# A hybrid decoder step on one core: sample outputs from the old states with eight buffers, the S5 output in two halves, and the SSD norm between other gate blocks

## What is computed

```
proj = rmsnorm(x) @ w_in                       # z, xBC, dt, u
xBC  = silu(causal_conv(xBC))                  # x, B, C of the SSD heads
y    = ssd(x, dt, A, B, C, D, h0)              # 16 heads of 64, state 128, chunks of 128 tokens
y_ssd = rmsnorm(y * silu(z)) * ssd_norm
y_s5 = s5(u, h0_re, h0_im)                     # 64 groups, diagonal complex state of 64
y_s5 = gelu(y_s5);  y_s5 = rmsnorm(y_s5 * sigmoid(y_s5 @ w_glu + b_glu)) * s5_norm
x    = x + concat(y_ssd, y_s5) @ w_out
x    = x + hier_moe(rmsnorm(x))                # top 2 of 32 experts, d_ff 512
```

```
h = exp(dt*A) * h0 + (dt*x) B^T                # 16 x 64 x 128 per sample: also an output
y = h C + D*x
```

## Time and profile before

| | us |
|---|---|
| median of 3 runs (lowest, highest) | 1232.8 (1232.26, 1233.92) |
| profiled execution, its own time | 1232.51 |
| its span, first to last instruction | 1230.7 |
| PE, DVE, ACT, POOL busy in the span | 1017.0, 399.5, 281.5, 299.4 |
| mean granted TensorE clock, share of full speed | 0.928 |

### The profile page before, as it was taken

The page is one execution under the profiler, slowest core; times in us unless marked ns, Lnnn a source line. Parts: engine busy times, 40 slices in busy tenths (PEclk is TensorE's granted clock), DMA queues, the critical chain, the costliest instruction groups (busy, mean ns, idle before and its releaser), DMA issues.

```text
span 1230.7 us, 16173 instructions
## 1 busy us (share of the span) xinstructions
PE 1017.0 (83%) x6140; PEld 692.2 (56%) x6141; DVE 399.5 (32%) x678; ACT 281.5 (23%) x554; POOL 299.4 (24%) x480
## 2 busy tenths in 40 slices
PE   5999999896999974699964999999976778976760
PEld 3888789675674763577743555555533434543430
DVE  3998374532423328651233101011000001000006
ACT  3125224530222604341121121121201111111102
POOL 1000788884014593035002001010100000000003
PEclk8999999897997896899985999999999999999895
DMA  5685341110057550415464999999999999999976
GB/s 214 241 137 84 75 106 36 37 52 16 29 121 160 188 154 18 161 70 205 171 255 167 384 389 383 389 394 386 394 401 398 400 405 395 385 389 402 390 271 214
DMA packets 83814, 291.19 MB, mean 237 GB/s; under 512 B 33460, under 2 KB 35380, under 8 KB 74940
## 3 DMA queue, kind: packets, MB, share of 16 engines
q1 hardware_dynamic: 69304, 252.97, 57.1%
q0 software_dynamic: 6944, 23.83, 6.3%
q10 hardware_dynamic: 7524, 13.83, 3.1%
HBM read 260.75 MB, written 27.59 MB: 234 GB/s over the span
## 4 chain that ended last, share of the span: by engine, by line
PE 48%; DMA 16%; POOL 15%; DVE 8%; issue 7%; SPq 3%; ACT 1%; DVEq 0%; ACTq 0%; POOLq 0%
DMA sb_arena<-w_up 11%; PE ps L860 9%; PE ps L618 8%; PE ps L957 7%; PE ps L950 7%; PE ps L971 6%; DMA sb_arena<-w_gate 4%; SPq L470 3%; POOL sb_rec L525 2%; POOL sb_rec L526 2%; POOL sb_arena L529 2%; POOL sb_arena L528 2%; POOL sb_rec L527 2%; PE ps L932 2%; PE ps L730 1%
## 5 line engine op out<-in xcount | busy, mean ns | idle before, releaser
L618 PE MATMUL ps<-sb_arena 128*128 128x264 f32 (+1 forms) x1152 | 272.9, 399 | 6.1 <-DVE sb_arena L1330 6.1
L618 PEld LDWEIGHTS ps<-sb_arena 128*128 128x128 f32 x1152 | 224.4, 196 | 55.4 <-issue 12.3
L950 PE MATMUL ps<-sb_arena 128*64 128x256 f32 x1152 | 138.4, 395 | 35.2 <-DMA sb_arena<-w_gate 28.3
L1708 DVE TENSOR_TENSOR sb_sst<-sb_sst,ps 128x256 f32<-128x256 f32 x36 | 15.2, 421 | 450.7 <-PE ps L957 414.0
L971 PE MATMUL ps<-sb_arena 128*64 128x512 f32 x576 | 131.5, 598 | 26.8 <-DVE sb_arena L1713 26.8
L957 PE MATMUL ps<-sb_arena 128*64 128x256 f32 x1152 | 132.9, 384 | 20.9 <-DMA sb_arena<-w_up 20.9
L950 PEld LDWEIGHTS ps<-sb_arena 128*64 128x64 f32 x1152 | 86.3, 143 | 98.4 <-DMA sb_arena<-w_gate 39.5
L957 PEld LDWEIGHTS ps<-sb_arena 128*64 128x64 f32 x1152 | 83.2, 138 | 66.6 <-DMA sb_arena<-w_up 27.1
L581 POOL COPY sb_idc<-sb_idx 64x1 int32 x36 | 6.4, 178 | 439.2 <-ACT sb_arena L1271 439.1
L971 PEld LDWEIGHTS ps<-sb_arena 128*64 128x64 f32 x576 | 38.1, 136 | 97.1 <-issue 61.7
L1274 ACT ACTIVATE sb_kxf<-ps 128x512 f32<-128x512 f32 x36 | 21.5, 597 | 310.5 <-PE ps L971 310.5
(11 more groups left out here) (270 smaller groups left out, 1205.4 us busy)
## 6 DMA issues: line engine op xcount, KB each, us to landing
sb_arena<-w_gate SPq DMA_DIRECT2D x32, 2048.0 KB, 35.0
sb_arena<-w_up SPq DMA_DIRECT2D x32, 2048.0 KB
sb_arena<-w_down SPq DMA_DIRECT2D x32, 2048.0 KB
sb_arena<-wi SPq DMA_DIRECT2D x28, 512.0 KB, 4.1
ye_scr<-sb_kxf ACTq DMA_DIRECT2D x72, 128.0 KB
sb_arena<-w_out SPq DMA_DIRECT2D x4, 2048.0 KB, 8.3
ye_scr<-sb_arena SPq DMA_DIRECT2D x2, 2048.0 KB, 11.9
sb_arena<-wglu SPq DMA_DIRECT2D x8, 512.0 KB, 4.9
```

The costliest lines, as they stand in the source:

```text
L618: last = mm(ps[:, b0 + h, 0:t1 - t0], ring[w % 3][:, k, :], src[:, k, t0:t1], start=k == 0, stop=k == KD - 1)
L950: last = mm(ps[64 * r:64 * r + 64, 0, 0:256], xt[:, k, :], Wg[s][:, k, 256 * r:256 * r + 256], start=k == 0, stop=k == KD - 1)
```

## The change

The output of a sample is formed from its old state: y = exp(dt*A) * (h0 C) + (C.B) * dt*x + D*x. VectorE multiplies the old state by C as soon as it is loaded; only then does GpSimd update the state in place (it waits for `smv_done` of the same sample). All eight states have buffers of their own, loaded at once; the first four lie where ScalarE later writes the sigmoids, which therefore wait for their stores, and the high part of `w_out` waits for the others.

B and C of the samples are transposed behind block 13, copied by ScalarE into a tile of 516 columns, to which VectorE adds C.B; ScalarE's queue stores them to a scratch tensor, and GpSimd's queue loads them broadcast to 128 partitions (8 x 516 floats each) behind the last state output, ahead of the states. Samples 0 and 1 stand on VectorE between chunks 3 and 4.

The S5 output is stored and loaded in halves of 32 groups, the first as soon as half of the additions are done. `Tm` is cleared by VectorE instead of GpSimd. ScalarE takes the exponentials of chunk 0 ahead of the last two SiLUs. The squares of the SSD norm stand behind the sigmoid of block 29 instead of 31, its partition sum behind block 31 instead of 33, and the high parts one block earlier.

The diff without declarations:

```diff
-        h0b = [part(20272 + 1024 * i, 8, NSTATE) for i in range(HB)]
+        h0b = [part((30832 if i < 4 else 16176) + 1024 * i, 8, NSTATE) for i in range(NS)]
+        bcf = part(26416, NS * BCW)
...
@@ sync
-            for w in range(22, 29):
+            for w in range(22, 26):
                 ring_load(w)
-            sp.wait_ge(y5_ev, 16)
...
+            def y_store(half):
+                sp.wait_ge(y5_ev, 8 * half + 8)
+                gs = slice(32 * half, 32 * half + 32)
+                for j in range(J):
+                    sp.dma_start(ydst[j][:, gs], Ug[16 * j:16 * j + 16, gs, 0:NC5]).then_inc(y5_st[half], 16)
+                sp.dma_start(ysdst[:, gs], Ug[0:16, gs, COL_S0:COL_S0 + NS]).then_inc(y5_st[half], 16)
...
+            y_store(0)
+            for w in range(26, 29):
+                ring_load(w)
+            y_store(1)
+            sp.wait_ge(y5_st[0], 16 * 9)
+            y_load(0)
+            sp.wait_ge(y5_st[1], 16 * 9)
+            y_load(1)
@@ gpsimd
-            pl.wait_ge(k_mm, 1)
-            nc.gpsimd.memset(Tm, 0.0).then_inc(t_zero, 1)
...
-            for b in range(HB):
-                pl.dma_start(h0b[b], hin[b]).then_inc(h0s_ld[b], 16)
+            pl.wait_ge(bc_st, 16)
+            pl.wait_ge(s5_out, 32)
+            pl.dma_start(bcf, bc_scr.rearrange("b c -> (b c)").partition_broadcast(P)).then_inc(bc_ld, 16)
             for b in range(NS):
-                hb = h0b[b % HB]
-                pl.wait_ge(bcs_ev, b + 2)
+                pl.dma_start(h0b[b], hin[b]).then_inc(h0s_ld[b // 4], 16)
+            pl.wait_ge(bc_ld, 16)
+            for b in range(NS):
+                hb = h0b[b]
                 link(nc.gpsimd.tensor_tensor(smu.rearrange("p (g i) n -> p g i n", g=2), bc(bcb[b][:, 0:2], 2, 4),
                                              bc(xds[:, :, b].rearrange("p (g i) -> p g i", g=2), 3, NSTATE), ALU.mult))
-                pl.wait_ge(h0s_ld[b % HB], 16 * (b // HB + 1))
+                pl.wait_ge(smv_done, b + 1)
                 link(nc.gpsimd.tensor_tensor(hb, hb, bc(eA[:, :, b], 2, NSTATE), ALU.mult))
...
-                if 1 <= b <= NS - HB:
...
@@ tensor
+            wide(13)
+            pe.wait_ge(silu_done, 4)
+            for i in range(4):
+                last = nc.tensor.transpose(ps[0:24, 7, i * P:(i + 1) * P], xcB[:, i, 4 * P:N], ident)
+            last.then_inc(bcs_mm, 1)
...
-            sample_bc()
             ssd_a(4)
-            pe.wait_ge(bcs_ev, 9)
             ssd_b(4)
...
-            for w in range(28, 34):
+            for w in range(28, 32):
                 wide(w)
             pe.wait_ge(sqt_done, 1)
             mean_square(sq, ms_done, None, 1)
-            for w in range(34, 36):
+            for w in range(32, 36):
                 wide(w)
@@ scalar
+            ac.wait_ge(bcs_mm, 1)
+            act_(btf[0:24, 0:512], ps[0:24, 7, :], ACT.Copy).then_inc(bcs_ev, 1)
...
+            ac.wait_ge(bcs_ev, 2)
+            ac.dma_start(bc_scr, btf[16:24]).then_inc(bc_st, 16)
...
+            segment_exp(0)
+            conv_silu(XBC - 2)
+            conv_silu(XBC - 1)
...
             for i in range(8):
+                if i % 4 == 0:
+                    ac.wait_ge(yraw_ld[i // 4], 16)
...
+                if w == 28:
+                    ac.wait_ge(h0s_st[0], 64)
...
-                if w == 31:
+                if w == 29:
                     ac.wait_ge(gt_done, 1)
                     for k in range(KD):
                         act_(sq[:, k, :], ySSD[:, k, :], ACT.Square).then_inc(sq_done, 1)
+                if w == 31:
+                    ac.wait_ge(h0s_st[1], 64)
+                    wo_high(0)
                 if w == 32:
-                    for s_ in range(HB):
-                        ac.wait_ge(h0s_st[s_], 32)
-                    wo_high(0)
+                    norm_root(0)
                 if w == 33:
-                    norm_root(0)
-                if w == 34:
                     high_parts(0, ySSD)
@@ vector
             conv(1)
+            dv.wait_ge(k_mm, 1)
+            V.memset(Tm, 0.0).then_inc(t_zero, 1)
             dv.wait_ge(k_ev, 1)
...
+            conv(5)
+            conv(6)
+            dv.wait_ge(bcs_ev, 1)
+            bt4 = btf[0:24, 0:512].rearrange("p (a n) -> p a n", a=4)
+            link(V.memset(btf[:, 512:BCW], 0.0))
+            tt(btp[0:24], bt4[:, 0:2], bt4[:, 2:4], ALU.mult)
+            V.tensor_reduce(btf[0:24, 512:514], btp[0:24], AX.X, ALU.add).then_inc(bcs_ev, 1)
+            conv(7)
+            conv(8)
...
-                dv.wait_ge(hn_done, b + 1)
+                dv.wait_ge(bc_ld, 16)
+                dv.wait_ge(h0s_ld[b // 4], 64)
                 tt(smv.rearrange("p (g i) n -> p g i n", g=2), bc(bcb[b][:, 2:4], 2, 4),
-                   h0b[b % HB].rearrange("p (g i) n -> p g i n", g=2), ALU.mult)
+                   h0b[b].rearrange("p (g i) n -> p g i n", g=2), ALU.mult)
...
+                if c == 3:
+                    sample_c(0)
+                    sample_c(1)
-            for b in range(NS):
+            for b in range(2, NS):
                 sample_c(b)
+            ysi = ysm[:].rearrange("p b i -> p i b")
+            tt(ysi, ysi, eA[:], ALU.mult)
+            dots = bcf.rearrange("p (b c) -> p b c", b=NS)[:, :, 512:514].rearrange("p b g -> p g b")
+            for g in range(2):
+                tt(dts[:, 4 * g:4 * g + 4], xds[:, 4 * g:4 * g + 4], bc(dots[:, g], 1, 4), ALU.mult)
+            tt(ysi, ysi, dts[:], ALU.add)
```

More of the change, by code:

```diff
@@ L65 @@
 WBUF = 3
-HB = 4
+BCW = 516
 E_LOOP = E // WBUF
@@ L94, in build @@
         y_scr = scratch("y_scr", [D, N])
+        bc_scr = scratch("bc_scr", [NS, BCW])
         x2_scr = scratch("x2_scr", [N, D])
@@ L274, in build @@
         raw_done, conv_done, silu_done = sem("raw_done"), sem("conv_done"), sem("silu_done")
-        h_done, y5_mm, y5_ev, y5_st = sem("h_done"), sem("y5_mm"), sem("y5_ev"), sem("y5_st")
+        h_done, y5_mm, y5_ev = sem("h_done"), sem("y5_mm"), sem("y5_ev")
+        y5_st = [sem(f"y5_st{i}") for i in range(2)]
         outs = sem("outs")
@@ L488, in _ @@
                 sp.dma_start(a["o_y"][t0:t0 + n, :], x1[i][0:n]).then_inc(outs, 16)
-            for s in range(HB):
-                sp.wait_ge(h0s_st[s], 32)
+            for s in range(2):
+                sp.wait_ge(h0s_st[s], 64)
             sp.wait_ge(s5_out, 32)
@@ L690, in _ @@
             last.then_inc(dtt_mm, 1)
-            for w in range(13, 17):
+            wide(13)
[3 more added lines that the diff above has]
+            last.then_inc(bcs_mm, 1)
+            for w in range(14, 17):
                 wide(w)
@@ L732, in state_outputs @@
                     last.then_inc(y5_mm, 1)
-            def sample_bc():
-                pe.wait_ge(y5_ev, 16)
-                for i in range(4):
-                    last = nc.tensor.transpose(ps[0:24, 2, i * P:(i + 1) * P], xcB[:, i, 4 * P:N], ident)
-                last.then_inc(bcs_mm, 1)
-                for b in range(NS):
-                    pe.wait_ge(bcs_ev, max(1, b))
-                    mm(ps[:, 3 - b % 2, :], cst[0:24, C_ID + 16 + b:C_ID + 17 + b].broadcast_to([24, P]), bts[0:24],
-                       start=True, stop=True).then_inc(bcs_mm, 1)
             def ssd_a(c):
@@ L1111, in _, with segment_exp @@
                 conv_silu(i - 2)
+            def segment_exp(c):
+                n = CH[c][1]
+                for i in range(4):
+                    ac.wait_ge(cb_mm, 4 * c + i + 1)
+                    act_(Lm[0:n, 4 * i:4 * i + 4, 0:n], ps[0:n, 2 + i % 2, 0:4 * n].rearrange("p (h l) -> p h l", h=4),
+                         ACT.Exp).then_inc(l_exp, 1)
+            segment_exp(0)
             conv_silu(XBC - 2)
@@ L1126, in b_tokens @@
                 act_(btok[0:n], ps[0:n, 6, 0:2 * P].rearrange("p (a q) -> p a q", a=2), ACT.Copy).then_inc(sa_eva, 1)
[L1128 to L1140 removed]
+            for c in range(5):
+                b_tokens(c)
+                if c:
                     segment_exp(c)
@@ L1470, in _ @@
             V.tensor_scalar(dav[:], dav[:], -1.0, None, ALU.mult).then_inc(dt_done, 1)
-            for i in range(5, 9):
-                conv(i)
+            conv(5)
[7 more added lines that the diff above has]
+            conv(8)
             dv.wait_ge(lc_mm, 16)
```

57 lines of the change are left out of this document (19 added, 38 removed).

## The result

The changed kernel is faster, by 1.6%. Four runs took 1211.55 to 1218.90 us, median 1216.8, against 1233.4 for the kernel before on the same chip: ratio 0.9835, 95% interval 0.9805 to 0.9864. The profiled execution took 1211.55 us with a span of 1209.0, so 21.0 less than before and 21.7 less of span. Forecast: 1206, range 1185 to 1220.

The account below looks back on a forecast made before the run. Bound: GpSimd's memset and S5 recurrence, then its eight-sample loop, ahead of the projection; expert loop and weight stream behind it unchanged. Projection at 479.7 against 506.55, 26.9 us earlier: 1232.5 - 26.9 = 1205.6, say 1206 us; range 1185 to 1220.

Parts of the forecast that it names:

- Tail: From GpSimd's last sample to the projection: last stores, W_out high part, subtraction, scalings, low parts; projection at 479.7 us.
- Recurrence: S5 recurrence on GpSimd: starts 10.9 us earlier without the memset; hold by VectorE's memset taken as 0, at most about 7.
- the recurrence gains little: Rival at the S5 recurrence: VectorE's memset holds it or TensorE arrives late; 7 us less gain, 1213 us; chance 0.11.
- TensorE ahead of the state outputs: Sample transposes and earlier exponentials: about 3 us late against a cover of 5.57 us idling, net taken as 0.4.
- Samples off TensorE: Broadcast matmuls vanish before chunk 4, which then waits for VectorE's state update at 365.3 us; gain there 19 us.
- Loads: Broadcast load and eight state loads ahead of sample 0: hidden, landing by 365 us at most; cost taken as 0.
- rival of a late broadcast: Broadcast load ahead of the states takes 50 us, VectorE stands 37 us with chunk 4 behind it; 1239 us; chance 0.07.
- Sample loop: GpSimd's samples from sample 2 on: end at 437.5 us, plus 14.3 lost to VectorE working beside it, so 451.8.
- GpSimd does not lose: First rival, at the sample loop: GpSimd's instructions fit between VectorE's, the 14.3 us fall away, 1191 us; chance 0.20.
- Other wait and S5 halves: First sigmoid's wait for four stores (TensorE idles 10 us) and S5 output in halves: both off the path, 0.
- the norm's place: SSD norm moved two gate blocks forward: keeps pace, nothing of it on the path to the projection, 0.

Follow-up runs that it names:

- e1: Changed kernel with the clearing of Tm given back to GpSimd, ahead of the recurrence; median 1217.8 us.
- e2: Changed kernel with Tm cleared by ScalarE, behind its evacuation of the S5 kernel; median 1205.2 us, ratio 0.976 to the kernel before.
- e3: Changed kernel with Tm cleared on VectorE by a one-input multiplication by zero in place of the memset; median 1209.6 us.
- e8: e2 with the high part of W_out waiting only for GpSimd's last read of B, the SSD high parts for the last four stores; median 1199.2 us.
- e10: e8 with three more samples (2 to 4) taken by VectorE inside chunk 4; median 1197.4 us, ratio 0.969 to the kernel before.
- e11: e10 with each sigmoid waiting only for the stores under it, and norm, low parts and W_out high part reordered; median 1192.8 us.
- e12: e11 with W_out's high part and the root placed earlier, partition sum behind block 33, low parts right behind the norm; median 1188.5 us.
- e4: Changed kernel with the SSD norm put back between its old gate blocks; median 1209.1 us.
- e7: Changed kernel whose VectorE waits with the gate until GpSimd has added the last sample; median 1222.3 us.
- e9: Changed kernel in which each sigmoid waits only for the stores of the buffers it writes over; median 1217.2 us.
- e6: Changed kernel with the S5 output stored by nine transfers and loaded by one, as before; median 1211.9 us.
- second profile: Profile of the changed kernel run once more without an edit, beside the other runs on one chip; median there 1213.9 us.

## Why the prediction was right, and where it was off

The sign, the range and the path were right: the last sample stores, the high part of W_out, the scalings and the low parts end last ahead of the projection, as forecast, with one link that the forecast had left out (*Tail*). The forecast for the projection was 479.7, measured 484.74: 5.0 us late. By its steps, each from the end of the one before:

| step | forecast | measured | off by |
|---|---|---|---|
| state outputs start | 279.7 | 286.55 | +6.9 |
| state outputs to VectorE's sample 2 | 112.0 | 113.1 | +1.1 |
| sample 2 to GpSimd's end | 60.1 | 57.6 | -2.5 |
| GpSimd's end to the projection | 27.9 | 27.4 | -0.5 |

That the total is off by less than the first step is partly luck: the 3.0 us of the last two have the other sign.

*Recurrence: the step that failed.* "Does it hold up GpSimd? ... I take 0; the upper bound is its whole length, about 7 us of the gain." It is the upper bound: 6.5 us, shown by e1, e2 and e3. The row I chose could not decide it: in the earlier trace rows GpSimd's step had begun first (200.50 against 200.57) and both ended within 0.01 us, so nobody could be seen waiting. The same trace had rows that could: where VectorE multiplied in the recurrence, a GpSimd step of 64 columns, 0.32 us elsewhere, took as long as the multiplication (kernel before; VectorE, then GpSimd):

```profile
240.94 1.23 DVE L1513 TENSOR_TENSOR sb_arena<-sb_arena 128x1024 f32<-128x1024 f32 x1
```

```profile
241.08 1.26 POOL L529 TENSOR_TENSOR sb_arena<-sb_arena,sb_rec 128x64 f32<-128x64 f32 x1
```

They are of a multiplication with two inputs and so do not prove it for a memset, but 0 was not what the trace suggested. On the path the hold costs less than its length, since TensorE was late too: of the 6.9 us, 3.8 are TensorE's wait for GpSimd (286.55 less 282.72). The rival "the recurrence gains little" named this mechanism and this price; it happened, and its 1213 us lies nearer to the measured times than 1206.

The Trainium skill (SBUF — State Buffer, Who interferes with whom) lets an instruction with at most one SBUF input hold GpSimd only in its two-port modes. The 4.44 us of e3, 0.54 ns a column where the gate takes 1.08, fit such a mode. The memset, with no input and 0.84 ns a column, held GpSimd too; the measurement decides.

*TensorE ahead of the state outputs* was taken as 0.4 us late. The wait for the SiLU took 2.92 us, as read from the earlier trace rows. Against the end of the S5 kernel matmuls TensorE was ready 2.8 us later than before, and 1.3 later in e1 and e3. The cover was the mistake: the idling of 5.57 us for the last SiLUs did fall to 0.44, but TensorE then idled 3.52 for VectorE at chunk 0 (line 1508), which the forecast did not have. 2.92 + 0.44 + 3.52 - 5.57 is the 1.3. The other 1.5 goes with TensorE's clock: between 167 and 187 us the granted clock was 0.91 in the changed kernel and 1.00 in e3. TensorE does not set the start in the changed kernel, but does in e2, e8, e10, e11 and e12: there this part gives 8.1 to 9.7 us without the hold, not 10.5.

*Samples off TensorE.* Chunk 4 at 372.87 follows VectorE's state update, with sample 0 behind it. The 1.1 us goes with TensorE's clock. In e4, whose edit works only later, sample 2 stands 110.4 behind SO, 2.7 less than here; 1.6 of that lie ahead of chunk 4 and 1.1 behind it. Chunk 4 stands behind 3.08 us of idling in both. In the 14 us that begin 86.0 behind SO, the granted clock was 0.65 of its 2.4 GHz in the changed kernel, so mostly at the lower level of 1.2, and 0.76 in e4; counted from chunk 4 on, it was 0.66 and 0.76 (windows, changed kernel and e4):

```profile
372.55:386.55 14.00, 13.50 (x50) 7.63 (x51) 11.30 (x13) 1.17 (x5) 10.74 (x6) 0.65 1.07 233
```

```profile
370.46:384.46 14.00, 13.82 (x55) 8.28 (x54) 9.74 (x11) 1.62 (x7) 12.34 (x6) 0.76 0.84 245
```

No run takes the clock away by itself, and none reverts the early broadcast or the eight buffers, so what these two gave is read from the traces.

*Loads.* Costed at 0 and measured 0; the rival of a late broadcast fell, at 10.9 us against the 9.1 of its nearest row and the 6.8 of the prediction's estimate. The row of 10.9 for the state loads was misread: it is the median of eight, of which the first four, beside the S5 store, took 13.3 to 16.7 us in the kernel before and the others 6.1 to 8.5. The cover was long enough all the same: the fourth state landed 6.3 us before VectorE asked.

*Sample loop.* 14.3 us were forecast for the two engines going one after the other (17.0 less a sixth is 14.2). Summed over GpSimd's operations of samples 2 to 7, what they take above 1.92, 1.91 and 2.34 us is 11.2. e7 gives 7.6 of it back, which the rival "GpSimd does not lose" (the first of the rivals, which the prediction once calls the second) would not. The size was off in the short operations: beside the gate GpSimd lost 4.3 of VectorE's 4.6 us, beside the five sample multiplies 3.6 of 6.1, beside the work behind the gate 3.3 of 6.3. That VectorE loses there instead can be seen: four of its small products are stretched beside GpSimd (last section). No run takes this apart further.

*Tail.* 27.4 against 27.9. "Ready earlier but stand behind that subtraction" is what the trace shows: the scalings begin at 470.16, GpSimd's subtraction ends at 472.83, and they end 5.4 us later. But they were earlier by 2.7 us only, for a link that was not in the sum: ScalarE takes the root of the norm behind the high part of W_out, and VectorE its reciprocal behind that, so that the scalings begin 6.3 us behind the end of the high part. By the chain of waits this is the path. The subtraction, 8.9 us, covers it, and the first scaling, beside it, takes 3.24 us where the others take 0.77. One reason was wrong: the high part of W_out lies on the broadcast B and C; what lies on the buffers of the last samples is the high part of the SSD output. The description of the kernel before has the same mistake. e8, which waits for each by itself, gains 6.6 us by it.

*Other wait and S5 halves.* Both 0 for the projection, by e9 and e6, and by e4 for the norm's place. TensorE idled 9.80 us, forecast 10. The halves were less than they look: the first half's store had landed at 321.6, but its load was issued at 373.6, since it stands behind the second half's stores in SP's list.

The medians, 1213.9 and 1216.8, stand 2 to 5 us above the profiled 1211.55. The second profile shows where such a difference lies: 1217.8 us, with the projection at 484.5 and 731.2 us behind it, where no part of the change works.

## What to carry to other kernels

Before moving a long VectorE write beside a chain of small GpSimd operations, find rows in which a GpSimd operation began well inside a long VectorE one; a row in which GpSimd began first, or 0.09 us behind, shows no hold. Here the same write on ScalarE cost GpSimd nothing. When a chain is shortened, lay out every engine that meets at its end: here the bound went from GpSimd's loop to TensorE's blocks (e10) and to VectorE behind GpSimd (e11) within 10 us.

## What was not expected of the hardware

A VectorE memset of 8192 float32 columns held a GpSimd step for 6.85 us, and a one-input multiplication of the same size, at twice the gate's rate, for 4.38; an activation of 7.05 us on ScalarE held none. Four of VectorE's small products of 32 to 64 columns, at most 0.27 us when alone, took 1.05 to 2.83 beside GpSimd's loop, the longest as long as the gate takes for 2600 columns. One that began 0.08 us behind GpSimd's addition ended with it (changed kernel; GpSimd, then VectorE):

```profile
423.05 2.34 POOL L574 TENSOR_TENSOR sb_arena<-sb_arena 128x1024 f32<-128x1024 f32 x1
```

```profile
423.13 2.34 DVE L1308 TENSOR_TENSOR sb_arena<-sb_arena,sb_pf 128x64 f32<-128x64 f32 x1
```

The weight stream ran at 378 to 391 GB/s in the same stretch of two executions of one kernel with all DMA engines busy; the whole stretch behind the projection differed by 7.0 us between them, more than several of the edits here are worth.
